# The modulation products of 20 of 24 blocks leave TensorE: GpSimd multiplies and adds the weight slices, TensorE sums over the rows

## The reference, cut to what matters

```python
def ada_modulation(cond, w, b):
    m = jax.nn.silu(cond) @ w + b        # (1024,) @ (1024, 6144)
    return jnp.split(m, 6, axis=-1)

for i in range(DEPTH):                   # DEPTH = 2
    sh1, sc1, g1, sh2, sc2, g2 = ada_modulation(c, w_ada[i], b_ada[i])
    csh1, csc1, cg1, csh2, csc2, cg2 = ada_modulation(c_ctx, w_ada[i], b_ada[i])
    h = modulate(x, norm_mix[i], sh1, sc1)
    ...                                  # mixer i, then
    x = x + g1[:, None, :] * o
    x = x + g2[:, None, :] * conv_ffn(modulate(x, norm_ffn[i], sh2, sc2), ...)
```

## Time and profile before

| | us |
|---|---|
| median of 3 runs (lowest, highest) | 4533.71 (4529.53, 4538.19) |
| the profiled execution, its time and its span | 4528.7, 4526.9 |
| PE busy | 4192.7 |
| DVE busy | 1904.7 |
| ACT busy | 1365.3 |
| POOL busy | 16.9 |

### The profile page before, as it was taken

How to read it: one execution, slowest core, us unless ns; L and a number is a source line. 1 busy time by engine, 2 the same in 40 slices (tenths; PEclk the granted TensorE clock), 3 DMA queues, 4 the chain that set the end, 5 groups by cost and what they waited for, 6 DMA issues and landing times.

```text
span 4526.9 us, 47676 instructions
## 1 busy us (share of the span) xinstructions
PE 4192.7 (93%) x19464; PEld 3042.8 (67%) x19464; DVE 1904.7 (42%) x3023; ACT 1365.3 (30%) x2259; POOL 16.9 (0%) x33
## 2 busy tenths in 40 slices
PE   7999889999987989999888999999998889998999
PEld 3766558888763545888766656578876666656887
DVE  1333125555442233655385532243436745214334
ACT  2222214222233333333233342232222344313222
POOL 0000000000000000000000000000000000000000
PEclk9989999999988989999899999999989999999999
DMA  4231013333210002333211112233322111222331
GB/s 150 66 103 57 28 56 95 93 119 100 89 58 24 19 10 60 94 93 94 78 59 47 38 56 91 77 87 99 89 78 79 47 45 38 84 84 70 100 96 61
DMA packets 381223, 329.32 MB, mean 73 GB/s; under 512 B 12304, under 2 KB 348688, under 8 KB 380880
## 3 DMA queue, kind: packets, MB, share of 16 engines
q1 hardware_dynamic: 378432, 314.89, 23.0%
q0 software_dynamic: 2576, 11.37, 0.8%
HBM read 324.14 MB, written 2.10 MB: 72 GB/s over the span
## 4 chain that ended last, share of the span: by engine, by line
PE 73%; DVE 7%; ACT 5%; issue 2%; DMA 0%; ACTq 0%; DVEq 0%
PE ps L398 57%; PE ps L409 3%; PE ps L411 3%; PE ps L410 3%; PE ps L517 2%; DVE WL L360 1%; ACT WH L352 1%; PE ps L1572 1%; ACT arena_m L1612 1%; DVE arena_m L1594 1%; PE ps L1402 1%; DVE arena_m L1589 1%; PE ps L580 1%; PE ps L1561 1%; DVE stage_b L565 1%
## 5 line engine op out<-in xcount | busy, mean ns | idle before, releaser
L360 DVE TENSOR_TENSOR WL<-ring,WH 128x2048 fp32r<-128x2048 f32 (+3 forms) x221 | 461.4, 2088 | 354.8 <-ACT WH L352 354.5
L352 ACT CAST WH<-ring 128x2048 fp32r<-128x2048 f32 (+3 forms) x221 | 384.0, 1738 | 478.8 <-PE ps L398 387.5
L398 PE MATMUL ps<-MH,WH 128*128 128x512 f32 x1024 | 398.5, 389 | 3.2 <-DVE WL L360 3.2
L398 PE MATMUL ps<-MH,WL 128*128 128x512 f32 x1024 | 398.4, 389 | 0.0
L398 PE MATMUL ps<-ML,WH 128*128 128x512 f32 x1024 | 398.4, 389 | 0.0
L409 PE MATMUL ps<-MH,WH 128*128 128x512 f32 x768 | 343.1, 447 | 13.1 <-DVE WL L360 13.1
L398 PE MATMUL ps<-IH,WH 128*128 128x512 f32 (+1 forms) x880 | 336.1, 382 | 0.0
L398 PE MATMUL ps<-IL,WH 128*128 128x512 f32 (+1 forms) x880 | 325.9, 370 | 0.0
L398 PE MATMUL ps<-IH,WL 128*128 128x512 f32 (+1 forms) x880 | 325.1, 369 | 0.0
L411 PE MATMUL ps<-MH,WL 128*128 128x512 f32 x768 | 309.8, 403 | 0.0
L410 PE MATMUL ps<-ML,WH 128*128 128x512 f32 x768 | 308.9, 402 | 0.0
(11 more groups left out here) (282 smaller groups left out, 6778.0 us busy)
## 6 DMA issues: line engine op xcount, KB each, us to landing
ring<-in_w_in SPq DMA_DIRECT2D x62, 1024.0 KB, 5.2
ring<-in_w_ada SPq DMA_DIRECT2D x48, 1024.0 KB, 8.4
ring<-in_ffn_w_up SPq DMA_DIRECT2D x88, 512.0 KB, 5.2
ring<-in_w_gu SPq DMA_DIRECT2D x88, 512.0 KB, 5.1
ring<-in_ffn_w_down SPq DMA_DIRECT2D x28, 768.0 KB, 4.5
ring<-in_w_down SPq DMA_DIRECT2D x28, 768.0 KB, 4.4
ring<-in_gla_w_in SPq DMA_DIRECT2D x8, 1024.0 KB, 9.5
ring<-in_w_out SPq DMA_DIRECT2D x8, 1024.0 KB, 8.8
```

What stands on the lines that cost most here:

```text
L352: nc.scalar.copy(split_slot(key, WH), raw_slot(key)).then_inc(act_done, mark("act", ("rounded", k)))
L360: nc.vector.tensor_tensor(split_slot(key, WL), raw_slot(key), split_slot(key, WH).bitcast(F32), ALU.subtract).then_inc(dve_done, mark("dve ...
L398: m = nc.tensor.matmul(out, l, r, start=(i == 0), stop=(i == len(pairs) - 1))
```

## The change

Blocks 0 to 3 stay as they were. For the other 20, GpSimd multiplies each row tile of a piece with the condition's value of its partition, for both streams, and adds it to a running sum of 128 x 512 per stream (`ada_sums`, which is `spare`). All GpSimd instructions wait for the one before them where they share the scratch tile `ada_tmp`. TensorE then sums over the partitions: for each of 4 x 2 columns of the result the sums' 128 columns are the stationary operand and a column of ones is the moving one. ACT has no part any more, VectorE's bias addition stays. A block's ring slots are freed by GpSimd. The sum on TensorE stands after the third and the sixth step of a head's projections. In the feed-forward the plan has the blocks after the up tiles in `ADA1`, and the sums stand at `ADA1_SUM`, that is each at the place of the next block's load. The staging buffer is 56 words per partition shorter, to make room for the scratch tile and the ones.

```diff
@@ -123,6 +123,8 @@
         mats = sb("mats", [P, len(MATS), P])
         cond = sb("cond", [P, DT, 32])
         sel = sb("sel", [P, 2])
+        ones = sb("ones", [P, 1])
+        ada_tmp = sb("ada_tmp", [P, 256])
         modv = sb("modv", [P, 2, 48, 2])
         gain = sb("gain", [P, 2, 2, 2, DT])
...
@@ -218,6 +221,8 @@
             return w.rearrange("(t p) n -> p t n", p=P)[:, :, a:b]
 
         plan = []
+        ADA1 = [0, 2, 4, 5, 7, 9, 11, 12, 14, 16, 18, 19]
+        ADA1_SUM = ADA1[1:] + [21]
         GATE_ORDER = [(0, 0), (2, 0), (1, 0), (0, 1), (2, 1), (1, 1)]
 
         def piece(key, parts, split=False):
@@ -249,8 +254,7 @@
                     for j in range(GROUP * g, min(GROUP * g + GROUP, FT)):
                         piece(("up", tag, j), [(0, cols(up, 128 * j, 128 * j + 128)),
                                                (128, cols(up, FF + 128 * j, FF + 128 * j + 128))], True)
-                        if j % 2:
-                            extra(j // 2)
+                        extra(j)
 
                 def downs(g):
                     rows = down[128 * GROUP * g:128 * min(GROUP * g + GROUP, FT), :]
@@ -262,10 +266,9 @@
                         downs(g - 1)
                 downs(FT // GROUP)
 
-            def ada1(c):
-                ada(1, c)
-                if c == FT // 2 - 1:
-                    ada(1, c + 1)
+            def ada1(j):
+                if j in ADA1:
+                    ada(1, ADA1.index(j))
 
             ffn("a0", io["ffn_w_up"][0], io["ffn_w_down"][0], ada1)
             dn = io["mla_w_down"][0]
@@ -501,8 +504,8 @@
             nc.scalar.wait_ge(dve_done, at(("res", key, n, t0)))
             if i >= 2:
                 nc.scalar.wait_ge(pe_done, at(("hsq_read", key, i - 2)))
-            elif ("ada_turned", 1, 10 + i) in counts.at and key == "n1":
-                nc.scalar.wait_ge(pe_done, at(("ada_turned", 1, 10 + i)))
+            elif key == "n1":
+                nc.scalar.wait_ge(pe_done, at(("ada_turned", 1, 11)))
             nc.scalar.activation(NSQ[:, i % 2, 0:tn], X[:, n, t0:t0 + tn], ACT.Square).then_inc(
                 act_done, mark("act", ("hsq", key, i)))
 
@@ -623,6 +626,50 @@
                 nc.scalar.wait_ge(pe_done, at(("ada_turned", l, c - 2)))
             nc.scalar.copy(ada_rows[:, c % 2, :], bank_of(("ada", l, c))).then_inc(
                 act_done, mark("act", ("ada_rows", l, c), ("free", ("ada", l, c))))
+
+        ada_sums = spare
+
+        def ada_order(l, c):
+            return 12 * l + c
+
+        def ada_pool(l, c):
+
+            if l == 0 and c == 4:
+                nc.gpsimd.wait_ge(act_done, at(("cond",)))
+                nc.gpsimd.wait_ge(pe_done, at(("ada_turned", 0, 3)))
+            elif l == 1 and c == 0:
+                nc.gpsimd.wait_ge(pe_done, at(("hms", "n0f", 0)))
+                nc.gpsimd.wait_ge(pe_done, at(("hms", "n0f", CTX)))
+            else:
+                nc.gpsimd.wait_ge(pe_done, at(("ada_turned", l, c - 1)))
+            for i in range(2):
+                key = (("ada", l, c), i)
+                n, loads_n = where[key]
+                nc.gpsimd.wait_ge(slot_loaded[n % SLOTS], loads_n)
+                w = raw_slot(key).rearrange("p (t n) -> p t n", n=256)
+                for k in range(DT):
+                    for s in range(2):
+                        acc = ada_sums[:, s, 256 * i:256 * i + 256]
+                        last = k == DT - 1
+                        if k == 0:
+                            m = nc.gpsimd.tensor_scalar(acc, w[:, k, :], cond[:, k, s:s + 1], None, ALU.mult)
+                        else:
+                            nc.gpsimd.wait_ge(pool_done, at(("ada_part", l, c, i, k if s else k - 1, 1 - s)))
+                            nc.gpsimd.tensor_scalar(ada_tmp[:, :], w[:, k, :], cond[:, k, s:s + 1], None, ALU.mult).then_inc(
+                                pool_done, mark("pool", ("ada_tmp", l, c, i, k, s)))
+                            nc.gpsimd.wait_ge(pool_done, at(("ada_tmp", l, c, i, k, s)))
+                            m = nc.gpsimd.tensor_tensor(acc, acc, ada_tmp[:, :], ALU.add)
+                        m.then_inc(pool_done, mark("pool", ("ada_part", l, c, i, k, s), *([used(key), ("ada_sum", l, c)] if last else [])))
+
+        def ada_sum_pe(l, c, bank=None):
+
+            nc.tensor.wait_ge(pool_done, at(("ada_sum", l, c)))
+            out = take(("ada_turned", l, c), bank)
+            for j in range(4):
+                for s in range(2):
+                    m = nc.tensor.matmul(out[:, 2 * j + s:2 * j + s + 1], ada_sums[:, s, 128 * j:128 * j + 128], ones[:, :],
+                                         start=True, stop=True)
+            m.then_inc(pe_done, mark("pe", ("ada_turned", l, c)))
 
         def ada_dve(l, c):
             nc.vector.wait_ge(pe_done, at(("ada_turned", l, c)))
...
@@ -806,8 +854,8 @@
         TILES = [[0, 1, 2, 3, 4, 5], [1, 0, 5, 4, 3, 2]]
         LAST = (GLA_C - 1, 0)
 
-        PROJ_PE = [[("g", 0), ("g", 1), ("q", 1)], [("q", 0), ("k", 1)], [("k", 0), ("v", 0), ("v", 1)],
-                   [("v", 2), ("v", 3), ("ada", 0)], [("v", 4), ("v", 5), ("ada", 1)], [("kt", 0), ("kt", 1), ("turn", 0)]]
+        PROJ_PE = [[("g", 0), ("g", 1), ("q", 1)], [("q", 0), ("k", 1)], [("k", 0), ("v", 0), ("v", 1), ("ada", 0)],
+                   [("v", 2), ("v", 3)], [("v", 4), ("v", 5)], [("kt", 0), ("kt", 1), ("ada", 1)]]
 
         def proj_pe(h, what, i):
 
@@ -831,10 +879,7 @@
                         [(H[:, k, 128 * i:128 * i + 128], w[:, k, :]) for k in range(DT)])
                 m.then_inc(pe_done, mark("pe", ("v", h, i), used((("gla_in", h), 1))))
             elif what == "ada":
-                ada_pe(0, 4 + 2 * h + i, spare_bank())
-            elif what == "turn":
-                for c in range(2):
-                    ada_turn_pe(0, 4 + 2 * h + c, spare_bank())
+                ada_sum_pe(0, 4 + 2 * h + i, spare_bank())
             else:
                 nc.tensor.wait_ge(dve_done, at(("KS", h, i)))
                 for half in range(2):
@@ -892,8 +937,6 @@
                 nc.scalar.wait_ge(pe_done, at(("v", h, i)))
                 nc.scalar.copy(gb["V", p][:, i, :], bank_of(("v", h, i))[:, 0:256]).then_inc(
                     act_done, mark("act", ("V", h), ("free", ("v", h, i))))
-            elif what == "ada":
-                ada_act(0, 4 + 2 * h + i)
             else:
                 for half in range(2):
                     nc.scalar.wait_ge(pe_done, at(("kt", h, i, half)))
@@ -902,7 +945,7 @@
                                        act_done, mark("act", ("KT", h, i), ("free", ("kt", h, i, half))))
 
         PROJ_DVE = [[("min", 0), ("min", 1), ("B", 0)], [("B", 1), ("QD", 0)], [("QD", 1), ("KI", 0)],
-                    [("KI", 1), ("KS", 0)], [("KS", 1)], [("ada", 0), ("ada", 1)]]
+                    [("ada", 0), ("KI", 1), ("KS", 0)], [("KS", 1)], [("ada", 1)]]
 
         def proj_dve(h, what, i):
             p = h % 2
@@ -2414,26 +2454,13 @@
             nc.vector.wait_ge(dve_done, at(("sg", l)))
 
 
-        def ada1_pe(c):
-            ada_pe(1, c)
-            if c:
-                ada_turn_pe(1, c - 1)
-            if c == FT // 2 - 1:
-                ada_pe(1, c + 1)
-                ada_turn_pe(1, c)
-                ada_turn_pe(1, c + 1)
-
-        def ada1_act(c):
-            ada_act(1, c)
-            if c == FT // 2 - 1:
-                ada_act(1, c + 1)
-
-        def ada1_dve(c):
-            if c:
-                ada_dve(1, c - 1)
-            if c == FT // 2 - 1:
-                ada_dve(1, c)
-                ada_dve(1, c + 1)
+        def ada1_pe(j):
+            if j in ADA1_SUM:
+                ada_sum_pe(1, ADA1_SUM.index(j))
+
+        def ada1_dve(j):
+            if j in ADA1_SUM:
+                ada_dve(1, ADA1_SUM.index(j))
 
         def nothing(c):
             pass
@@ -2446,6 +2473,8 @@
             for i, (key, parts, split) in enumerate(plan):
                 if i >= SLOTS and plan[i - SLOTS][2]:
                     sp.wait_ge(dve_done, at(("slot_used", i - SLOTS)))
+                elif i >= SLOTS and plan[i - SLOTS][0][0][0] == "ada" and plan[i - SLOTS][0][0][1:] >= (0, 4):
+                    sp.wait_ge(pool_done, at(("slot_used", i - SLOTS)))
                 elif i >= SLOTS:
                     sp.wait_ge(pe_done, at(("slot_used", i - SLOTS)))
                 width = parts[-1][0] + parts[-1][1].shape[2]
@@ -2626,6 +2655,10 @@
         def _(pool):
             start_pool()
 
+            for c in range(4, 12):
+                ada_pool(0, c)
+            for c in range(12):
+                ada_pool(1, c)
             pool.wait_ge(dve_done, at(("hnormed", "n1")))
             stage_load("axial", [(tabs, io["rope"][:, 0]), (X[:, :, 0:CTX], io["memT"])])
             for l in range(2):
```

More of the change, by code:

```diff
@@ L51 @@
 SPLITS = 2
-STAGE = 14756
+STAGE = 14700
 GROUP = 3
@@ L185, in build @@
         dve_done = ctx.enter_context(nc.semaphore("dve_done"))
```

(8 more changed lines are left out.)

## The result

| | before | after |
|---|---|---|
| median, us | 4533.7 (4 runs) | 5002.8 (4 runs, 5001.6 to 5013.5) |
| ratio | | 1.104, 95% interval 1.1021 to 1.1059 |
| the profiled execution: time, span | 4528.7, 4526.9 | 5013.5, 5011.7 |
| attention stage, 96 us to the last turn or sum | 330.3 | 466.9 |
| first feed-forward, last squares of the norm before it to the last turn or sum | 579.0 | 914.2 |

10.4% slower, where 4708 us, 3.8% (the prediction writes 3.9), was forecast and the range ended at 7.9%. The two stages grew by 136.6 and 335.2 us. GpSimd's first load after the second norm comes 472.9 us later than before, and the median grew by 469.1, so both stages together are the effect. The profiled execution of the changed kernel is 10.7 us above its median: behind that load it took 3218.5 us where the one before took 3206.7, and the other three executions are 10 to 12 us shorter in all.

The account below looks back on a forecast made before the run. TensorE, busy 93% of the span, was taken to bound the kernel. The profiled 4528.7 us + 60 (attention stage) + 114 (feed-forward) gave 4703, or 4708 us against the median, 3.9% slower; range 4580 to 4890.

Parts of the forecast that it names:

- Removed and added on TensorE: Both stages: products and turns removed save 82.6 us, column sums add 15 and 24; TensorE alone would gain 43 us.
- The price of a GpSimd instruction: In a GpSimd block: 0.67 us an instruction, taken between 0.34 and 0.93, so 60 instructions make 40 us.
- T: Time GpSimd takes for one block, 60 instructions with their hand-overs; forecast 40 us, between 20 and 56.
- Where T lies: Both stages: TensorE waits at sums for GpSimd, and next loads stand behind held slots; +60 and +114 us.
- event walk: The prediction's account of the stops in both stages, redone with another T; at 40 us it gave +60 and +114.
- Attention stage: Second sums stall 16.7 us three times, 20.8 in the first head; plus 7 for clock, less 18 gained: +60 us.
- Feed-forward: First feed-forward: 55 us at sums, 57 at late weights, 27 of lower clock, less 25 gained: +114 us.
- Rival 1: Both stages: VectorE and GpSimd block each other, T 48 or 50 us; 4820 us in all, chance 0.21.
- The clock's share: Feed-forward: lower clock after stops costs 19 us at seven load stalls and 8 at five stalled sums.
- The eight stops at weights: Feed-forward: TensorE stalls for weights loaded late behind held slots, the longest 9.1 us at up 5; 57 us in all.
- Rivals 2 and 4: GpSimd at VectorE's price, T 27, 4595 us, chance 0.17; GpSimd hides wholly, about 4505 us with T 10, chance 0.05.
- Rival 3: Both stages: GpSimd's upper bound is true, 0.93 us an instruction, T 56; +133 and +286, 4953 us, chance 0.08.

## Why the prediction was wrong

- **Removed and added on TensorE**: right in size, and small beside the stops. The 8 sums of a block cost 1.84 us at full clock, near the 1.9 taken, and 3.57 at the 12 places with a stop.
- **The price of a GpSimd instruction** is the step that failed: "I take 0.67 us, just over the middle of the two prices (0.34 and 0.93)". It is 59.2 / 60 = 0.99 us: 0.922 and 0.722 alone by 32 and 28 make 49.7 us, the hand-overs of 0.085 add 5.1, VectorE 4.4. My upper end was a DMA issue, which has nothing to do with arithmetic on 256 columns; the truth lay beyond it. Nothing in the trace bounded this price from above, and I should have let the range say so instead of giving T of 56 and more a chance of 0.08. The Trainium skill (GPSIMD Engine Reference, Performance versus the Vector engine) had the price of the addition: its 2.6 cycles at 1.2 GHz are, as an estimate, 2.17 ns an element, and the runs show 2.1. Its one to 1.8 cycles for one input fit the copy (0.83 ns, 1.0 cycle) but not the product with a scalar, which took 3.0 cycles here (2.5 ns), and the product with the broadcast column took 2.0 where its two-input price would be 2.6; there the measurement decides.
- **Where T lies** held in the sum, and in part by luck. The event walk with the measured T, and with nothing else changed, gives 4603, 4842 and 5006 us at 28.8, 49.5 and 59.2 us a block; measured were 4608, 4848 and 5003. But it gives +36, +99 and +156 for the attention stage, where the traces have +26, +71 and +137, and +38, +214 and +321 for the feed-forward, where they have +42, +236 and +335. The two errors have opposite signs. That the cost follows T is shown; the 5 us by which the totals agree are not a measure of how good the walk is.
- **Attention stage**: too long in the walk. Its 7.5 us at the first sums for T = 48 mean 45.5 us of TensorE's work ahead of each; the traces have 52 us there, also in the kernel with half the products, so the stops are 7.2 to 8.5 us where the walk has some 14. The second sums wait 22 to 25 us and that of the first head 39.9, near the forecast. But at this T it is not the load that sets them, as the prediction had it: GpSimd waits for none there, and a second sum waits for a whole block, 57 to 59 us there, less 32 to 35 us of TensorE's work.
- **Feed-forward**: too short in the walk. Missing was the stop inside the down pieces, 15 us by the run with the later split, and the 7 us ahead of the first up tile that are told under Rival 1. The clock's share was of the right kind: 27 us were forecast at T = 40, and at 59.2 the helper's matmuls took 41 us more and the sums 31 where 24 was taken. (The eight stops at weights in the prediction add up to 56, not 57, which changes nothing.)
- **Rival 1**, VectorE and GpSimd blocking each other: true as a mechanism, wrong as a size. I gave it 8 us of a block, it was 4.4: VectorE's two-SBUF-input time is spread over 914 us, not 567, and the longer the stage the smaller its share (11% of T with half the products and with the broadcast product, 7% here). In the feed-forward GpSimd's instructions ran 59 us over their shortest times, and 55 of these stand in instructions beside VectorE's operations with two SBUF inputs. In the changed kernel GpSimd's instruction beside VectorE's L1315 took 1.51 instead of 0.93 us:

```profile
1013.81 0.93 POOL L658 TENSOR_SCALAR ada_tmp<-ring,cond 128x256 f32<-128x256 f32 x1
...
1015.06 1.30 DVE L1315 TENSOR_TENSOR conv<-conv 128x768 f32<-128x768 f32 x1 [0.91 <-ACT conv L1290]
1015.64 1.51 POOL L658 TENSOR_SCALAR ada_tmp<-ring,cond 128x256 f32<-128x256 f32 x1
```

  It also works the other way, in one place where TensorE waits for VectorE: the norm ahead of the feed-forward, beside which GpSimd makes the first block. VectorE's group there, before (667 to 696 us) and in the changed kernel (807 to 843):

```profile
L554 DVE SCALAR_TENSOR_TENSOR HL<-stage_b,modv,HH 128x512 fp32r<-128x512 f32 x8 | 6.0, 750 | 0.1
...
L557 DVE SCALAR_TENSOR_TENSOR HL<-stage_b,modv,HH 128x512 fp32r<-128x512 f32 x8 | 8.0, 1001 | 0.0
```

  TensorE waits 9.3 us for it instead of 5.9 and reaches its first up tile 35.2 us after the last squares instead of 28.4. In the kernel with the attention stage alone it is 28.4 again. The prediction had named such a wait as a sign of being wrong; it is there, and worth 7 us.

  The Trainium skill (SBUF — State Buffer, Who interferes with whom) has it as a lock between GpSimd and VectorE operations with two SBUF inputs or copies in a two-port mode, and none for operations with at most one SBUF input outside such a mode. The three cases timed agree with it.
- **Rivals 2 and 4** needed an instruction at or below VectorE's price; none of the forms timed is there but the copy (0.40). **Rival 3** came nearest: it said 4953 at T = 56, and T was 59.2.

## What to carry to other kernels

Before work is given to an idle engine, time its very instruction in its very form alone: that one number decided 300 us here (5003 less the 4703 of the walk at T = 40), and another form of the same product was worth 155. Then compare the time of one unit with the busy engine's own work between two meeting points, not with the engine's idle time in the whole, and count what stands in order behind the slot and behind the wait. And look first at the places: leaving all products on TensorE and moving the blocks apart gave 0.45%, offloading them cost 10.4%.

## What the runs showed of the hardware that I had not expected

- GpSimd's product with a scalar (2.5 ns a column) is slower than its addition of two tensors (2.1 ns), and slower than the same product with the column broadcast as a second tensor (1.67 ns, from 612 and 1892 ns at 256 and 1024 columns). A copy takes 0.83 ns.
- A GpSimd operation of 0.92 us takes 2.84 beside VectorE operations of 2.3 us with two SBUF inputs, and those become 2.54: they take turns.
- It works both ways: VectorE's operation of 0.75 us took 1.00 beside GpSimd, and TensorE, which waited for it, started 7 us later.
- Matmul records went down by 480 and TensorE's busy time up by 54 us: in the feed-forward the same matmuls took 545 us at a mean granted clock of 0.80, and 504 at 0.98.
